# Key turns and key products stay in the stage that forms the systems; values, queries and scores move under the small blocks' transfers

## The chip, the core and the metric

The kernel runs on one core of a Trainium2 chip. A time is the device time of one execution in microseconds; three executions of the kernel before took 2998.97, 3002.99 and 3005.89 us, median 3002.99. Five engines work side by side, each in the order of its own list of instructions: TensorE (PE in the rows; its weight loads are PEld), VectorE (DVE), ScalarE (ACT), GpSimd (POOL) and SyncE (SP), which issues most of the DMA transfers. They wait for one another on semaphores. An instruction that waits holds back everything behind it on its engine.

## The reference, cut to what matters

A first block (a gated delta rule and a pooling mixer on 512 tokens and 256 context tokens, width 1024) and two transformer layers behind it. The change lies in the delta rule, which runs over 8 heads of 128 channels, forward and backward:

```python
hn = _rms_norm(h, gain) * (1 + scale) + shift
proj = jnp.einsum('bld,dp->blp', hn, w_in)
qkv = jax.nn.silu(_short_conv(qkv, conv_w))       # five taps
q, k = _l2_norm(q), _l2_norm(k)
...
# _gated_delta_rule, in chunks of tokens
decay = jnp.exp(jnp.where(incl, g[..., :, None] - g[..., None, :], -jnp.inf))
a_mat = jnp.where(strict, jnp.einsum('bhncd,bhnsd->bhncs', kb, k) * decay, 0.0)
sol = lax.linalg.triangular_solve(eye + a_mat, rhs, left_side=True, lower=True,
                                  unit_diagonal=True)
qk = jnp.einsum('bhncd,bhnsd->bhncs', q, k) * decay
...
def step(state, inp):
    v_new = u_i - jnp.einsum('bhcd,bhdv->bhcv', w_i, state)
    o_i = (jnp.einsum('bhcd,bhdv->bhcv', q_i, state)
           + jnp.einsum('bhcs,bhsv->bhcv', qk_i, v_new))
    state = state * jnp.exp(gl_i)[..., None, None] + jnp.einsum('bhcd,bhcv->bhdv', k_i, v_new)
```

## The kernel before, in words

The heads go in four groups of two (`GROUPS`), and each group has six tiles of 128 tokens (`TILES`): four of the sequence, two of the context. Channels lie on the partitions, so keys, values and queries have to be turned, tile by tile, before tokens lie there. All large products are made of three matmuls on split numbers (L149 to L151: high by high, high by low, low by high); the weights come in slabs by DMA, ScalarE rounds a slab (`split_hi`, L137) and VectorE makes the rest (`split_lo`, L142).

A group G runs through these stages.

1. *Systems.* For each tile TensorE sums the rows of the decay (L1589, L1591 in `rows`), turns keys and, in the first four tiles, queries into bank 3 and values into bank 7 (`turn_heads`, L1573 and L1578), multiplies keys by keys and by queries into bank 5 or 6 (`products`, L1601), and runs one part of a projection. ScalarE makes the exponentials (`decays`, L861), squares and copies of the turned keys, and the copy of the values (`squares`, L847 to L852). VectorE sums the squares (`norms`), multiplies scores (`scores`, kept as `qkd`) and systems (`system`, L1194, kept as `bt`).
2. *Small blocks.* SyncE sends the diagonal blocks of the systems to memory (L636) and back in another shape (L641); VectorE inverts them there in 15 rounds of four operations (`invert`, L1234 and L1240); SyncE sends the inverses out (L648) and in (L653). Meanwhile TensorE runs the rest of `fill`, the projections of group G+1 (part by part, `take(fill, 99)`), then `busy`, sixteen matmuls of no result (L1416), and then `turn_inverse` (L1616) waits for the blocks.
3. *Sweep.* 18 steps (`STEPS_LEVEL`) of turn, product (L1654) and correction make the whole inverse out of the blocks. From step 13 on TensorE takes one part of `later`, the projections of group G+2, after each step. `conv_ops` on VectorE (L1152) and `act_head`/`act_center` on ScalarE (L768 to L791) make the short convolution of group G+1 between these steps.
4. *Scan.* Six steps over the tiles, the first within the sweep: `against` and `answer` multiply the state, VectorE makes the residual (L1284) and the new state (L1295), TensorE `renew`, `grow` (L1679, L1688) and `inner` (the scores by the new values, L1719), with parts of `later` between them. At the end TensorE waits for the outputs (`oa_ready`, `ot_ready`) and goes to the next group.

The order is written out by hand. Semaphores hold the dependences: `vs_ready` counts the values that ScalarE has copied out of bank 7, and the next tile's value turn waits for it; `bt_ready` counts the systems; `qkd_ready` the scores, which are first read in `inner`; `bounce` counts the transfers of the blocks, and `dve_step` VectorE's own steps. In the stage of the small blocks ScalarE runs `act_raw`, `act_head`, `act_center` for group G+1 (L137, L768 to L791; in the last group a gate, `act_gate`, stands there), then the root of the key norms (L877, behind a table load) and the clearing of banks 5 and 6 (L880), which hold the key products till then.

GpSimd multiplies the values and the keys for the scan (L1835 to L1840), once the group's values are there.

Of the kernel before, what the change touches and what calls it, by code (L numbers as in the profile page):

```python
# [9 lines left out]
F32 = mybir.dt.float32  # L10
# [36 lines left out]
EPS = 1e-6  # L47
# [107 lines left out]
def make_layer_memory(nc, K, at):  # L155

    def put(name, shape, dtype=F32, where=None):
# [4 lines left out]
        if where is None:  # L162
# [112 lines left out]
HALF_SEMS = {"sum_made": ("tk_ready", 24), "sumh_ready": ("tv_ready", 24), "suml_ready": ("hsq_ready", 24), "plain_ready": ("hss_ready", 24),  # L275
             "diff_made": ("arg_ready", 24), "diffh_ready": ("dec_ready", 24), "diff_ready": ("kk_ready", 24),
# [125 lines left out]
NORM_STEPS = 2 * TILES + 1  # L402
# [52 lines left out]
def make_first_memory(nc, K, at):  # L455
# [64 lines left out]
    at += 2048  # L520

# [18 lines left out]
    K.junk = put("square_junk", [128, 4, 128])  # L540
    at += 2048
# [69 lines left out]
def delta_block(K):  # L611
# [224 lines left out]
    def act_group(act, G):  # L836
# [4 lines left out]
        def squares(t):  # L841
            n = TILES * G + t
            w = 4 if t < 4 else 2
            act.wait_ge(S.tk_ready, n + 1)
            if n > 0:
                act.wait_ge(S.hss_ready, n)
            nc.scalar.activation(K.junk[:, 0:w, :], pb[3][:, 0:128 * w].rearrange("p (c v) -> p c v", v=128), ACT.Square)\  # L847
                .then_inc(S.hsq_ready, 1)
            nc.scalar.activation(K.ks[:, t, 0:2, :], pb[3][:, 0:256].rearrange("p (c v) -> p c v", v=128), ACT.Copy)\
                .then_inc(S.kt_ready, 1)  # L850
            act.wait_ge(S.tv_ready, n + 1)
            nc.scalar.activation(K.vs[:, t, :, :], pb[7][:, 0:256].rearrange("p (j v) -> p j v", v=128), ACT.Copy)\  # L852
                .then_inc(S.vs_ready, 1)

        def decays(t):
            n = TILES * G + t
            act.wait_ge(S.arg_ready, n + 1)
            act.wait_ge(S.bt_ready, n - 1 + CREDIT)
            for c in range(4):
                at = 8 * (c // 2) + 2 * G + c % 2  # L860
                last = nc.scalar.activation(K.decs[t % 2][:, c, :], pb[4][:, 128 * c:128 * c + 128], ACT.Exp,  # L861
                                            bias=K.ncum[:, t, at:at + 1])
            last.then_inc(S.dec_ready, 1)
# [72 lines left out]
        for i in range(STEPS_LEVEL):  # L936
# [7 lines left out]
            if more and i in (0, 12, 16):  # L944
                act_head(act, G + 1, {0: 1, 12: 2, 16: 3}[i])
            if more and i in (1, 13, 17):
                act_center(act, G + 1, {1: 3, 13: 4, 17: 5}[i])
        for n, (f, b, x) in enumerate(scan_steps()):
# [4 lines left out]
            if x is not None:  # L953
                state_out(x, (f, b))
            if more and n == 3:
# [207 lines left out]
    def dve_group(dve, G):  # L1163
# [5 lines left out]
        def norms(t):  # L1169
            n = TILES * G + t  # L1170
            w = 4 if t < 4 else 2
            dve.wait_ge(S.hsq_ready, n + 1)
            nc.vector.tensor_reduce(K.ssq[:, t, 0:w], K.junk[:, 0:w, :], AX.X, ALU.add).then_inc(S.hss_ready, 1)
            dve.wait_ge(S.hss_ready, n + 1)
            step.link(nc.vector.tensor_scalar(K.ssq[:, t, 0:w], K.ssq[:, t, 0:w], EPS, None, ALU.add))
            step.link(nc.vector.reciprocal(K.n2[:, t, :], K.ssq[:, t, 0:2]))

        def scores(t):
            n = TILES * G + t
            dve.wait_ge(S.dec_ready, n + 1)  # L1180
            dve.wait_ge(S.kk_ready, n + 1)
            for j in range(2):
                ins = nc.vector.scalar_tensor_tensor(out=quad(K.qkd[:, t, :, :])[:, :, j, :], in0=quad(K.decs[t % 2][:, :, :])[:, :, j, :],
                                                     scalar=K.n2[:, t, j:j + 1],
                                                     in1=wide(pb[5 + t % 2][:, 256 + 128 * j:384 + 128 * j], 1, 2),
# [3 lines left out]
        def system(t):  # L1189
            n = TILES * G + t  # L1190
            dve.wait_ge(S.dec_ready, n + 1)
            dve.wait_ge(S.kk_ready, n + 1)
            for j in range(2):
                ins = nc.vector.scalar_tensor_tensor(out=quad(K.bt[t][:, :, :])[:, :, j, :], in0=quad(K.decs[t % 2][:, :, :])[:, :, j, :],  # L1194
# [6 lines left out]
        for t in range(TILES):  # L1201
            norms(t)
            if t < 4:
                scores(t)
# [4 lines left out]
                                wide(K.n2[:, :, :], 2, 2), ALU.mult).then_inc(S.tail_ready, 1)  # L1209
        step.link(nc.vector.tensor_scalar(K.fq[:, 2 * G:2 * G + 2, :].rearrange("p j t -> p t j"), K.ssq[:, 0:4, 2:4], 128 * EPS, None,  # L1210
                                          ALU.mult))
        if more:
            take(conv, 4)
# [42 lines left out]
        for i in range(STEPS_LEVEL):  # L1256
# [13 lines left out]
            take(conv, 1)  # L1270
# [42 lines left out]
        for n, (f, b, x) in enumerate(scan_steps()):  # L1313
# [8 lines left out]
            if n == 4 and more:  # L1322
# [229 lines left out]
    def pe_group(pe, G, fills):  # L1552
        s, v = DN_SLAB + 6 * (G + 1), DN_EVIC + 6 * (G + 1)
        fill, later = fills[G], islice(fills[G + 1], 14 if G + 1 < GROUPS else 16)
# [10 lines left out]
        def turn_heads(t):  # L1565

            n = TILES * G + t
            lo = 128 * t
            if t > 0:
                pe.wait_ge(S.kt_ready, n)  # L1570
            for c in range(4 if t < 4 else 2):
                src = keys(G, c) if c < 2 else queries(G, c - 2)
                last = nc.tensor.transpose(pb[3][:, 128 * c:128 * c + 128], src[:, lo:lo + 128], K.ident[:, :])  # L1573
            last.then_inc(S.tk_ready, 1)
            if t > 0:
# [1727 lines left out]
```

## Time and profile before

| | |
|---|---|
| median of three executions | 3002.99 us |
| the profiled execution | 3003.65 us |
| its span, first to last instruction | 3001.3 us |
| granted TensorE clock, mean | 0.989 |
| TensorE busy | 2901.6 us, 97% of the span |
| VectorE, ScalarE, GpSimd busy | 71%, 46%, 15% |

The share of an engine is an average over all stages. TensorE's is so high that the span is read from its side: what it runs, and where it stands idle. A granted clock of 1.00 is the upper of TensorE's two levels (2.4 GHz), 0.50 the lower (1.2 GHz). The other engines are read only where TensorE waits for them. The four groups' system stages begin at 121.98, 240.02, 356.62 and 475.49 us of the span; the two layers that the change does not touch begin after the first block.

### The profile page before, as it was taken

What the parts mean: (1) busy time and instruction counts of PE and PEld (TensorE: products, weight loads), DVE (VectorE), ACT (ScalarE), POOL (GpSimd) and SP (SyncE); (2) the same over time, 40 slices, a digit from 0 to 9 for tenths busy, and PEclk for the clock granted to TensorE, in tenths of its full rate; (3) what the DMA queues carried; (4) which work ended last, traced back from release to release, by engine and by line L of the source; (5) the groups of instructions that cost most, each with busy time, mean ns of one, the idle gap of its engine ahead of it and who ended that gap; (6) DMA issues with size and microseconds to landing.
All of it is one profiled execution on the core that took longest, in us unless ns stands there. A gap on an engine that the chain in (4) does not pass through costs nothing.

```text
span 3001.3 us, 50795 instructions
## 1 busy us (share of the span) xinstructions
PE 2901.6 (97%) x18548; PEld 2497.8 (83%) x18548; DVE 2128.3 (71%) x3193; ACT 1394.4 (46%) x2305; POOL 455.7 (15%) x356
## 2 busy tenths in 40 slices
PE   7999999889999999999999999999999999999998
PEld 3888888777799988777799988799888777899886
DVE  5677676455699745987799745899547886899545
ACT  3645555454366522334456522566323334566322
POOL 0113112184600010000300012100110000200012
PEclk9999999999999999999999999999999999999998
DMA  6212022123222322232323323233223222323322
GB/s 258 64 42 63 24 55 61 34 84 116 98 98 98 105 96 81 93 96 77 99 98 106 107 97 109 72 105 111 88 88 97 94 78 85 105 98 112 106 95 73
DMA packets 97244, 275.09 MB, mean 92 GB/s; under 512 B 35712, under 2 KB 36864, under 8 KB 95760
## 3 DMA queue, kind: packets, MB, share of 16 engines
q1 hardware_dynamic: 94016, 267.89, 27.3%
q10 hardware_dynamic: 2768, 4.25, 0.5%
q8 instruction: 92, 1.51, 0.2%
q0 software_dynamic: 320, 1.05, 0.1%
q14 instruction: 48, 0.39, 0.0%
HBM read 267.88 MB, written 5.28 MB: 91 GB/s over the span
## 4 chain that ended last, share of the span: by engine, by line
PE 84%; DVE 6%; ACT 3%; issue 2%; DMA 0%; ACTq 0%; DVEq 0%; POOL 0%; SPq 0%; POOLq 0%
PE bank L149 16%; PE bank L151 16%; PE bank L150 16%; PE bank L2053 8%; PE bank L2054 8%; PE bank L2055 8%; PE bank L1616 1%; DVE weights_lo L142 1%; ACT weights_hi L137 1%; PE bank L1679 1%; PE bank L1630 1%; PE bank L2544 1%; PE bank L2565 1%; PE bank L2555 1%; DVE short_conv L1152 1%
## 5 line engine op out<-in xcount | busy, mean ns | idle before, releaser
L142 DVE TENSOR_TENSOR weights_lo<-weights_raw,weights_hi 128x1024 fp32r<-128x1024 f32 (+2 forms) x258 | 396.9, 1538 | 326.5 <-ACT weights_hi L137 323.2
L137 ACT ACTIVATE weights_hi<-weights_raw 128x1024 fp32r<-128x1024 f32 (+2 forms) x250 | 285.3, 1141 | 432.1 <-PE bank L151 425.1
L149 PE MATMUL bank<-x_hi,weights_hi 128*128 128x512 f32 x832 | 336.8, 405 | 4.7 <-DVE x_lo L1943 3.0
L151 PE MATMUL bank<-x_hi,weights_lo 128*128 128x512 f32 x832 | 326.4, 392 | 0.0
L150 PE MATMUL bank<-x_lo,weights_hi 128*128 128x512 f32 x832 | 325.3, 391 | 0.0
L2053 PE MATMUL bank<-sum_hi,block_hi 128*128 128x256 f32 x960 | 270.9, 282 | 4.6 <-ACT bank L2205 3.7
L150 PE MATMUL bank<-hidden_lo,weights_hi 128*128 128x512 f32 x704 | 273.9, 389 | 0.0
L149 PE MATMUL bank<-hidden_hi,weights_hi 128*128 128x512 f32 x704 | 273.9, 389 | 0.0
L151 PE MATMUL bank<-hidden_hi,weights_lo 128*128 128x512 f32 x704 | 273.9, 389 | 0.0
L2054 PE MATMUL bank<-sum_lo,block_hi 128*128 128x256 f32 x960 | 270.5, 282 | 0.0
L2055 PE MATMUL bank<-sum_hi,block_lo 128*128 128x256 f32 x960 | 269.2, 280 | 0.0
L149 PE MATMUL bank<-normed_hi,weights_hi 128*128 128x512 f32 (+1 forms) x512 | 196.2, 383 | 10.6 <-ACT grid L1004 7.0
L2053 PE MATMUL bank<-x_hi,block_hi 128*128 128x256 f32 x640 | 181.9, 284 | 13.7 <-DVE block_lo L2357 7.7
L149 PEld LDWEIGHTS bank<-x_hi,weights_hi 128*128 128x128 f32 x832 | 157.2, 189 | 39.3 <-issue 4.9
L150 PE MATMUL bank<-normed_lo,weights_hi 128*128 128x512 f32 (+1 forms) x512 | 188.1, 367 | 0.0
L151 PE MATMUL bank<-normed_hi,weights_lo 128*128 128x512 f32 (+1 forms) x512 | 188.0, 367 | 0.0
L2053 PEld LDWEIGHTS bank<-sum_hi,block_hi 128*128 128x128 f32 x960 | 181.3, 189 | 5.8 <-ACT bank L2205 4.4
L151 PEld LDWEIGHTS bank<-x_hi,weights_lo 128*128 128x128 f32 x832 | 156.8, 188 | 34.2
L150 PEld LDWEIGHTS bank<-x_lo,weights_hi 128*128 128x128 f32 x832 | 157.2, 189 | 31.1 <-issue 1.7
L2055 PEld LDWEIGHTS bank<-sum_hi,block_lo 128*128 128x128 f32 x960 | 181.5, 189 | 0.0
L2054 PEld LDWEIGHTS bank<-sum_lo,block_hi 128*128 128x128 f32 x960 | 181.2, 189 | 0.0
L2055 PE MATMUL bank<-x_hi,block_lo 128*128 128x256 f32 x640 | 180.9, 283 | 0.0
(436 smaller groups left out, 7323.8 us busy)
## 6 DMA issues: line engine op xcount, KB each, us to landing
raw_pair<-w_ff1in SPq DMA_DIRECT2D x42, 1024.0 KB, 4.9
raw_pair<-w_ff2in SPq DMA_DIRECT2D x42, 1024.0 KB, 4.9
weights_raw<-w_mix SPq DMA_DIRECT2D x72, 512.0 KB, 3.5
weights_raw<-w_ff1out SPq DMA_DIRECT2D x32, 704.0 KB, 4.1
weights_raw<-w_ff2out SPq DMA_DIRECT2D x32, 704.0 KB, 4.1
weights_raw<-w_tail SPq DMA_DIRECT2D x42, 512.0 KB, 3.6
mod_weights<-w_mod SPq DMA_DIRECT2D x6, 2048.0 KB, 16.7
weights_raw<-w_dn SPq DMA_DIRECT2D x24, 512.0 KB, 3.7
```

The lines of the kernel that those rows point to most:

```text
L137: nc.scalar.activation(K.wh[:, slot, 0:cols], K.raw[:, slot, 0:cols], ACT.Copy).then_inc(S.wh_ready, 1)
L142: nc.vector.tensor_tensor(K.wl[:, slot, 0:cols], K.raw[:, slot, 0:cols], K.wh[:, slot, 0:cols].bitcast(F32), ALU.subtract).then_inc(S.raw_ ...
L149: nc.tensor.matmul(out, K.wh[:, slot, a:b], xh, start=start, stop=False)
L150: nc.tensor.matmul(out, K.wh[:, slot, a:b], xl, start=False, stop=False)
L151: return nc.tensor.matmul(out, K.wl[:, slot, a:b], xh, start=False, stop=stop)
L1152: ins = nc.vector.scalar_tensor_tensor(out=acc[:, base + lo:base + hi], in0=K.hv[i][:, base + lo + k - 2:base + hi + k - 2], scalar=K.wk[: ...
L1616: last = nc.tensor.transpose(pb[turn_bank(i)][:, 128 * q:128 * q + 128], K.e[:, q, t, :], K.ident[:, :])
L1630: last = nc.tensor.matmul(pb[3 + i % 2][own, 64 * q:64 * q + 64], K.bl[t][own, q, :] if i < STEPS_FIRST else K.bt[t][own, q, own], K.dd[ow ...
L1679: last = nc.tensor.matmul(pb[scan_bank(n, d)][:, part(j)], K.e[:, c, t, :], K.rr[:, c, :] if n else K.vs[:, t, j, :], start=True, stop=True)
L2053: nc.tensor.matmul(out, hi[:, a], x[0][:, k, :], start=start and k == 0, stop=False, skip_group_check=True)
L2054: nc.tensor.matmul(out, hi[:, a], x[1][:, k, :], start=False, stop=False, skip_group_check=True)
L2055: last = nc.tensor.matmul(out, lo[:, a], x[0][:, k, :], start=False, stop=(k == 3), skip_group_check=True)
```

## The change

The stage of the systems keeps the row sums, the key turns (`turn_keys`) and the products of keys by keys. The turns of the values, the turns of the queries (now into bank 7 beside the values) and the products of keys by queries (now into banks 3 and 4) come after the sixth tile, each tile followed by one part of a projection. Therefore:

- ScalarE copies values and squares queries (`values`) after its first steps for group G+1, and not tile by tile.
- VectorE sums the squared queries between convolution steps, and multiplies the scores after the inversion. The decays of the four sequence tiles stay in `qkd` until then.
- TensorE waits for the last value copy before the sixteen filler matmuls and for the scores before it turns the inverse.
- The waits for the outputs at a group's end move into the next group, before the first key product and before the first value turn.
- In the first two groups 20 parts of later projections are kept for the sweep and the scan, not 14 (in the third 16, before 14; in the last 16 as before); the sweep takes them from step 12 on, the scan at other places. Convolution steps on VectorE and ScalarE move within the sweep and the scan, on VectorE ahead of the new state.

```diff
@@ act_group
+        def values(t):
+            n = TILES * G + t
             act.wait_ge(S.tv_ready, n + 1)
+            if t < 4:
+                if t > 1:
+                    act.wait_ge(S.dve_step, (NORM_STEPS + SMALL_STEPS) * G + 2 * TILES + t - 1)
+                nc.scalar.activation(K.qsq[:, t % 2, :, :], pb[7][:, 256:512].rearrange("p (j v) -> p j v", v=128), ACT.Square)\
+                    .then_inc(S.hsq_ready, 1)
             nc.scalar.activation(K.vs[:, t, :, :], pb[7][:, 0:256].rearrange("p (j v) -> p j v", v=128), ACT.Copy)\
                 .then_inc(S.vs_ready, 1)
...
             act_center(act, G + 1, 1)
         else:
             act_gate(act, 1)
+        act.wait_ge(S.bt_ready, TILES * G + TILES + CREDIT)
+        for t in range(TILES):
+            values(t)
         act.wait_ge(S.dve_step, (NORM_STEPS + SMALL_STEPS) * G + 2 * TILES)
         nc.scalar.activation(K.knorm[:, :, :], K.ssq[:, :, 0:2], ACT.Sqrt).then_inc(S.knorm_ready, 1)
-        act.wait_ge(S.bt_ready, TILES * G + TILES + CREDIT)
@@ dve_group
         for t in range(TILES):
             norms(t)
-            if t < 4:
-                scores(t)
             system(t)
...
+        for t in range(4):
+            take(conv, 1)
+            query_sums(t)
...
-        if more:
-            take(conv, 4)
         split_lo(dve, s + 2, 0, 1024)
...
-            take(conv, 8)
         else:
             split_lo(dve, s + 5, 1, 1024)
+        dve.wait_ge(S.kk_ready, (TILES + 1) * (G + 1))
+        for t in range(4):
+            scores(t)
+        take(conv, 2)
...
-            take(conv, 1)
+            take(conv, 1 if i < STEPS_INNER else 2)
...
             if n < 5:
+                take(conv, 3 if n < 3 else 2)
                 new_state(n, (f, b))
-                take(conv, 3 if n < 3 else 2)
@@ pe_group
-        fill, later = fills[G], islice(fills[G + 1], 14 if G + 1 < GROUPS else 16)
+        fill, later = fills[G], islice(fills[G + 1], 20 if G + 2 < GROUPS else 16)
...
         for t in range(TILES):
             rows(t)
-            turn_heads(t)
+            turn_keys(t)
+            if t == 0 and G > 0:
+                pe.wait_ge(S.oa_ready, 4 * G)
             products(t)
             take(fill, 2 if G == 0 and t < 2 else 1)
+        if G > 0:
+            pe.wait_ge(S.ot_ready, 8 * G)
+        for t in range(TILES):
+            turn_rest(t)
+            take(fill, 1)
+            if t == 2:
+                pe.wait_ge(S.kt_ready, TILES * (G + 1))
+                pe.wait_ge(S.dec_ready, TILES * (G + 1))
+            if t > 1:
+                query_products(t - 2)
         take(fill, 99)
+        pe.wait_ge(S.vs_ready, TILES * (G + 1))
         busy(pe, pb[turn_bank(0)], 8)
+        pe.wait_ge(S.qkd_ready, 4 * (G + 1))
         for i in range(3):
             turn_inverse(i)
...
-            if i > STEPS_INNER:
+            if i >= STEPS_INNER:
                 take(later, 1)
```

The order of TensorE's list in the second group, from the row sums of its sixth tile on; `head_v` holds the values, `keys_queries` keys and queries, the three rows L149 to L151 are one part of a projection. Before:

```order
L1589 MATMUL bank<-sum_rows_141,row_pairs 128x128 [waits dec_ready]
L1589 MATMUL bank<-sum_rows_141,row_pairs 128x128 x3
L1591 MATMUL bank<-not_included,identity_r 128x512
L1573 MATMUL bank<-identity,keys_queries_175 128x128 [waits kt_ready]
L1573 MATMUL bank<-identity,keys_queries_175 128x128
L1578 MATMUL bank<-identity,head_v 128x128 [waits vs_ready]
L1578 MATMUL bank<-identity,head_v 128x128
L1601 MATMUL bank<-keys_queries_175 128x128 [waits bt_ready]
L1601 MATMUL bank<-keys_queries_175 128x128
L149 MATMUL bank<-normed_hi,weights_hi 128x256
```

From here on the projections ran without other work in between. After the change the list goes on, behind the key products of the same tile, with:

```order
L1630 MATMUL bank<-keys_queries_175 128x128
L149 MATMUL bank<-normed_hi,weights_hi 128x512
L150 MATMUL bank<-normed_lo,weights_hi 128x512
L151 MATMUL bank<-normed_hi,weights_lo 128x512
L1594 MATMUL bank<-identity,head_v 128x128 [waits ot_ready]
L1594 MATMUL bank<-identity,head_v 128x128
L1598 MATMUL bank<-identity,keys_queries_175 128x128 x2
L149 MATMUL bank<-normed_hi,weights_hi 128x512
L150 MATMUL bank<-normed_lo,weights_hi 128x512
L151 MATMUL bank<-normed_hi,weights_lo 128x512
L1594 MATMUL bank<-identity,head_v 128x128 [waits vs_ready]
L1594 MATMUL bank<-identity,head_v 128x128
```

The value turns left the tile and stand behind the projection part, four transposes at a time for values and queries, with the wait on the copied values at the second of them.

ScalarE's list in the same group, from the squared keys of the sixth tile on; `head_k`, `head_q` and `short_conv` belong to the convolution of the next group. Before:

```order
L847 ACTIVATE square_junk<-bank 128x256 [waits hss_ready,tk_ready]
L849 ACTIVATE decayed_keys<-bank 128x256
L852 ACTIVATE values<-bank 128x256 [waits tv_ready]
L137 ACTIVATE weights_hi<-weights_raw 128x1024 [waits slab_done,raw_full1]
L768 ACTIVATE head_k<-bank 128x512 [waits slab_done]
L770 ACTIVATE head_k<-bank 128x256
L791 ACTIVATE short_conv_206<-head_q,short_taps 128x512 [waits evac,head_ready]
L791 ACTIVATE short_conv_207<-head_k,short_taps 128x768 [waits evac,head_ready]
L877 ACT_TABLE_LOAD
L877 ACTIVATE key_norm<-head_squares 128x12 [waits dve_step]
```

Every tile's values were copied right behind its keys. Now, from the same place:

```order
L849 ACTIVATE decayed_keys<-bank 128x256
L137 ACTIVATE weights_hi<-weights_raw 128x1024 [waits slab_done,raw_full1]
L769 ACTIVATE head_k<-bank 128x512 [waits slab_done]
L771 ACTIVATE head_k<-bank 128x256
L792 ACTIVATE short_conv_207<-head_q,short_taps 128x512 [waits evac,head_ready]
L792 ACTIVATE short_conv_208<-head_k,short_taps 128x768 [waits evac,head_ready]
L857 ACTIVATE query_squares<-bank 128x256 [waits tv_ready,bt_ready]
L859 ACTIVATE values<-bank 128x256
L857 ACTIVATE query_squares<-bank 128x256 [waits tv_ready]
L859 ACTIVATE values<-bank 128x256
```

All six value copies stand behind the five steps for the next group and ahead of the table load and the key norms.

## Rows read from the trace of the kernel before

**Rows 1.** Page, busy time, share of the span and instructions of each engine.

```profile
PE 2901.6 (97%) x18548; PEld 2497.8 (83%) x18548; DVE 2128.3 (71%) x3193; ACT 1394.4 (46%) x2305; POOL 455.7 (15%) x356
```

**Rows 2.** Timeline, TensorE: start us, us, line, out<-in, count [idle before <-releaser].

```profile
255.68 0.66 PE L1589 MATMUL bank<-sum_rows,row_pairs 32*128 32x128 f32 x4
...
256.82 0.38 PE L1578 MATMUL bank<-identity,head_v 128*128 128x128 f32 x2
257.04 0.61 PE L1601 MATMUL bank<-keys_queries 128*128 128x128 f32 x4
257.40 0.36 PE L149 MATMUL bank<-normed_hi,weights_hi 128*128 128x256 f32 x1
```

**Rows 3.** Timeline, TensorE, end of the projections.

```profile
288.69 1.95 PE L1416 MATMUL bank<-ones 128*128 128x128 f32 x16
290.47 1.47 PE L1616 MATMUL bank<-identity,inverse 128*128 128x128 f32 x12
```

**Rows 4.** Timeline, SyncE's DMA queue, 262 to 290: time of issuing.

```profile
279.56 0.30 SPq L648 DMA_DIRECT2D inverse_blocks<-small_inverse  x1
283.38 2.60 SPq L653 DMA_DIRECT2D inverse<-inverse_blocks  x4
286.03 1.44 SPq L625 DMA_DIRECT2D weights_raw<-w_dn  x2
```

**Rows 5.** Waits, TensorE, 290.4 to 356.7: us in total, times, longest.

```profile
PE bank L1679 <- DVE residual L1284: 2.3, 3, 1.2
PE bank L1589 <- issue: 0.9, 1, 0.9
PE bank L1719 <- ACT new_values L922: 0.6, 1, 0.6
```

**Rows 6.** Windows: length, each engine's busy us (instructions), granted clock, DMA share, GB/s.

```profile
240.00:243.40 3.40, 3.38 (x23) 2.85 (x24) 0.63 (x1) 2.36 (x8) 3.14 (x3) 1.00 0.27 70
...
357.20:360.60 3.40, 3.40 (x16) 3.22 (x16) 0.90 (x2) 2.17 (x7) 2.50 (x3) 0.50 0.27 82
360.60:364.00 3.40, 3.40 (x25) 2.86 (x25) 2.89 (x6) 1.41 (x5) 1.34 (x2) 1.00 0.23 36
473.20:480.00 6.80, 5.91 (x28) 5.34 (x26) 1.73 (x4) 4.03 (x11) 3.66 (x4) 0.50 0.14 35
```

**Rows 7.** Timeline, TensorE, one projection part in the sweep.

```profile
322.90 0.48 PE L149 MATMUL bank<-normed_hi,weights_hi 128*128 128x512 f32 x1
323.22 0.39 PE L150 MATMUL bank<-normed_lo,weights_hi 128*128 128x512 f32 x1
323.45 0.40 PE L151 MATMUL bank<-normed_hi,weights_lo 128*128 128x512 f32 x1
323.77 0.45 PE L1654 MATMUL bank<-inverse,product 64*64 64x64 f32 x8
```

**Rows 8.** Timeline, ScalarE, from the sixth tile's exponentials on.

```profile
256.80 1.14 ACT L861 ACTIVATE decay_odd<-bank,log_beta_less_sum 128x128 f32<-128x128 f32 x4 [0.65 <-PE bank L1591]
...
258.34 0.42 ACT L852 ACTIVATE values<-bank 128x256 f32<-128x256 f32 x1
258.61 1.10 ACT L137 ACTIVATE weights_hi<-weights_raw 128x1024 fp32r<-128x1024 f32 x1
...
260.91 1.00 ACT L791 ACTIVATE short_conv<-head_k,short_taps 128x768 f32<-128x768 f32 x1
261.92 1.28 ACT L877 ACT_TABLE_LOAD   x1
...
263.34 1.10 ACT L880 ACTIVATE bank<-identity 128x512 f32<-128x512 f32 x2
```

**Rows 9.** Timeline, VectorE: last system, inversion, a split, convolution steps.

```profile
259.41 0.87 DVE L1194 SCALAR_TENSOR_TENSOR system<-decay_odd,key_square_inverse,bank 128x256 f32<-128x256 f32 x2
...
269.53 0.32 DVE L1234 TENSOR_TENSOR small_product<-small_system,small_inverse 48x30 f32<-48x30 f32 x2 [0.41 <-DMA small_system<-system_blocks]
...
284.58 2.51 DVE L142 TENSOR_TENSOR weights_lo<-weights_raw,weights_hi 128x1024 fp32r<-128x1024 f32 x1 [3.92 <-ACT weights_hi L137]
...
330.56 1.80 DVE L1152 SCALAR_TENSOR_TENSOR short_conv<-head_v,short_taps,short_conv 128x511 f32<-128x511 f32 x3
```

**Rows 10.** Timeline, GpSimd, its last multiplication of the group.

```profile
286.08 3.63 POOL L1840 TENSOR_TENSOR decayed_keys<-decayed_keys,tail_by_square 128x1536 f32<-128x1536 f32 x1
```

More of the change, by code:

```diff
@@ L539, in make_first_memory @@
     K.decs = [K.dec, put("decay_odd", [128, 4, 128])]
-    K.junk = put("square_junk", [128, 4, 128])
-    at += 2048
+    K.junk = put("square_junk", [128, 2, 128])
+    at += 3072
     end = at
@@ L954, in act_group @@
                 state_out(x, (f, b))
+            if more and n == 1:
+                act_center(act, G + 1, 5)
             if more and n == 3:
@@ L1319, in dve_group @@
             if n < 5:
+                take(conv, 3 if n < 3 else 2)
                 new_state(n, (f, b))
-                take(conv, 3 if n < 3 else 2)
-            if n == 4 and more:
+            elif more:
                 split_lo(dve, s + 6, 0, 1024)
@@ L1577, in turn_heads, with query_products @@
             for j in range(2):
-                last = nc.tensor.transpose(pb[7][:, 128 * j:128 * j + 128], K.hv[HEAD_SLABS.index((2, j))][:, lo:lo + 128], K.ident[:, :])
-            last.then_inc(S.tv_ready, 1)
+                last = nc.tensor.transpose(pb[7][:, 128 * j:128 * j + 128], K.hv[HEAD_SLABS.index((2, j))][:, 128 * t:128 * t + 128],
+                                           K.ident[:, :])
+            if t < 4:
+                for j in range(2):
+                    last = nc.tensor.transpose(pb[7][:, 256 + 128 * j:384 + 128 * j], queries(G, j)[:, 128 * t:128 * t + 128],
+                                               K.ident[:, :])
+            last.then_inc(S.tv_ready, 1)
+        def query_products(t):
+            for j in range(2):
+                a = 256 * (t % 2) + 128 * j
+                last = nc.tensor.matmul(pb[3 + t // 2][:, a:a + 128], keys(G, j)[:, 128 * t:128 * t + 128],
+                                        queries(G, j)[:, 128 * t:128 * t + 128], start=True, stop=True)
+            if t == 3:
+                last.then_inc(S.kk_ready, 1)
         def rows(t):
@@ L1597, in products @@
                 pe.wait_ge(S.bt_ready, n - 1 + CREDIT)
-            lo = 128 * t
             for j in range(2):
-                key = keys(G, j)[:, lo:lo + 128]
+                key = keys(G, j)[:, 128 * t:128 * t + 128]
                 last = nc.tensor.matmul(pb[5 + t % 2][:, 128 * j:128 * j + 128], key, key, start=True, stop=True)
-                if t < 4:
-                    last = nc.tensor.matmul(pb[5 + t % 2][:, 256 + 128 * j:384 + 128 * j], key, queries(G, j)[:, lo:lo + 128],
-                                            start=True, stop=True)
             last.then_inc(S.kk_ready, 1)
@@ L1741, in pe_group @@
                 against(n, d, t)
-            if x is None:
-                take(later, 1)
-            else:
+            if x is not None:
                 answer(n, x, tiles)
+            take(later, 1)
             if n == 1:
@@ L1749, in pe_group @@
                 renew(n, d, t)
-            take(later, 2)
+            take(later, 2 if n in (2, 3, 4) else 1)
             if n < 5:
@@ L1753, in pe_group @@
                     grow(n, d, t)
-            if x is not None:
-                if x == 0:
-                    pe.wait_ge(S.qkd_ready, 4 * G + 4)
+            if x is None:
+                take(later, 1)
+            else:
                 inner(n, x, tiles)
-        pe.wait_ge(S.oa_ready, 4 * G + 4)
-        pe.wait_ge(S.ot_ready, 8 * G + 8)
     def pe_tail(pe):
+        pe.wait_ge(S.oa_ready, 4 * GROUPS)
+        pe.wait_ge(S.ot_ready, 8 * GROUPS)
         for i, (kind, m) in LATE:
```

63 lines of the change are left out of this document (31 added, 32 removed).

## The prediction

> **What bounds the kernel.** I read the page's engine shares first. TensorE is busy in 97% of the span [rows 1], so the time is its instructions plus the holes between them; another engine counts only where it makes a hole or a slower clock. I then read one of the four head groups, the second, in order of time; the others have the same pattern. All offsets below count from 255.68, where TensorE begins the row sums of that group's sixth and last tile [rows 2].
>
> After that tile TensorE runs projection products of the next group without a hole until 288.69, sixteen filler products until 290.47, and then turns the inverse [rows 3]. No idle time stands before 290.47, so the small blocks were back by then: VectorE's inversion ended at 279.56, the block loads were issued by 285.98 [rows 4]. The transfers are hidden today. The reader should look for holes elsewhere, and the view of waits has them: in the group's sweep TensorE stands idle 2.3 us for residuals, 0.6 for new values and 0.9 at the border to the next group [rows 5]. After two of the borders the granted clock is at 0.50, the lower of the two levels, once for 3.4 us and once for 6.8; in such a stretch 16 matmuls ran where the next 3.4 us held 25 [rows 6].
>
> **The change part by part.** TensorE's matmuls are the same in number and shape; only their order changes. So I add up holes, breaks and clock.
>
> *The shorter stage.* Two value turns, two query turns and two query products leave each of the first four tiles, two value turns each of the last two. That is no gain: TensorE still has to run them before it turns the inverse, and it was TensorE, not the transfers, that arrived there last.
>
> *The new wait.* Values share one bank, so the second tile's value turn waits until ScalarE has copied the first. In the last tile TensorE reaches the projection part at +1.72; less 0.22 for the value turns that left [rows 2] it is +1.50. One part of a projection takes 0.87 (322.90 to 323.77) [rows 7], the first turn of values and queries (four transposes, twice 0.22) 0.44, a second part 0.87: TensorE wants the second turn at +3.68. ScalarE has its exponentials at +1.12, then two copies, then a weight split, the copy of the next group's key projection and two centre steps, and ends these at 261.92, which is +6.24; without the value copy that stood among them (0.27, 258.34 to 258.61) it is +5.97 [rows 8]. Only then come the first query squares (0.26, like the copy) and the first values (0.42): +6.65. The hole is 6.65 - 3.68 = 3.0 us. Queued behind the waiting turn are all later turns, the query products and 37 parts of projections. Later tiles alternate without a hole worth counting: TensorE's 1.31 to 1.75 us a tile cover ScalarE's 0.7. In the last group a gate with a table load stands in place of the copies and centres; I take 3.0 there too. Four groups: 12.0 us. The bounds are 2.2 (ScalarE one step earlier) and 3.9 each.
>
> *Breaks in the projections.* Three products at the drain's pitch take 0.69 (323.22 to 323.45 is 0.23), a part by itself takes 0.87 [rows 7], so a part set between other work costs up to 0.18 that it does not cost in a row. The change breaks out six more parts a group under the transfers and in the sweeps 7, 7, 4 and 3: 45 places. At 0 to 0.18 each that is 0 to 8.1; what follows them is of other kinds than in the row, so I take 0.15: 6.8 us.
>
> *The transfers' and the scores' chains, at nothing.* TensorE leaves the value stage at 6.65 + 1.31 + 2 x 1.75 + 2 x 1.53 = +14.5, runs 32 parts of 0.69 (+36.6) and the filler of 1.78 (+38.4). The inversion today starts on its data at 269.53, +13.85 [rows 9]; now it stands on VectorE behind a weight split whose first half ScalarE makes only after the last values (+13.8), the table load, norms and bank clearing (2.52, 261.92 to 264.44) and 1.10 for itself [rows 8]: +17.4, with VectorE's half +18.6. Its 10.0 us and about 9.0 for the blocks' way out and in (between 6.4 and 10.9 by rows 3 and 4) give +37.6. So the head start of the shorter stage is lost on that wait, and the blocks arrive 0.8 before TensorE. The scores now stand after the inversion and after a split that needs the fifth projection, done 5.5 before the drain ends (+31.1): ScalarE 1.1, VectorE 1.2 to 2.5, eight score operations at 0.43 (the systems' two took 0.87 [rows 9]) end at +36.9 to +38.2. TensorE's new wait on them costs nothing while it arrives at +38.4, and whatever exceeds this if it comes sooner.
>
> VectorE's split took 2.51 us at 284.58 [rows 9], and GpSimd's last multiplication began at 286.08 and ended at 289.71 [rows 10]: the two disturb each other, and the scores now fall in just that time. The Trainium skill (SBUF — State Buffer, section "SBUF: two separate sides") says that GpSimd and VectorE hold one port pair by turns, for a whole instruction, and that of VectorE's instructions those in a two-port mode or with two SBUF inputs need it. A score has one input from PSUM, so by that rule it is not held, and the sum stays; without the rule the second rival below would be as likely as not.
>
> *The sweep.* Of the 3.8 us of holes named above, each understated by the 0.16 by which a matmul's recorded end overlaps the next start (256.82 + 0.38 against 257.04 [rows 2]), five times: 4.6 us. The convolution steps on VectorE now run before the new state instead of between it and the next residual (three of them took 1.80 [rows 9]), the fifth step gets two parts, and the waits at the border go. Left over: about 1.6 at the first scan step, where two convolutions instead of one precede each residual (0.6 more, twice over), and 0.5 for a copy and a centre on ScalarE that move into its busiest steps (0 to 1.8; a centre is 1.00 [rows 8]). Net -2.5 in groups one and two; in the third the parts run out before the fifth step, -1.5; in the last, which has 16 parts as before but none in the fifth step, +0.6 by the same count. Together -5.9 us, bounds -11 and +1.
>
> *The clock.* The three low stretches at the borders lost 9 of 25 matmuls in 3.4 us, 1.2 each: -3.7 if the holes before them go. But a 3.0 us hole is longer than any single hole at those borders (1.2 the longest [rows 5]), so I expect one low stretch in each group after it: 4 x 1.2 = +4.8.
>
> Sum: 12.0 + 6.8 - 5.9 - 3.7 + 4.8 = +14.0 us. The profiled execution took 3003.65, 0.66 above the median of 3002.99 and inside the runs' 2998.97 to 3005.89; so 3017.0 on the median's scale.
>
> **Rivals.**
> 1. *Not slower: the wait at the second value turn does not arise,* since ScalarE has room to spare (46% busy). Then 12.0 and its 4.8 of clock go: 14.0 - 16.8 = -2.8, 3000.2. It decides where ScalarE's first value copy ends before +3.7. Against it: ScalarE works in order and its row from 258.61 to 261.92 has no idle time. Chance 0.13, a part of it below 2997.
> 2. *The scores come last.* If GpSimd holds them, they start when its multiplications end, 10.1 us after the inversion (289.71 against 279.56 [rows 4, 10]): +38.7, done at +42.2, 3.8 later than TensorE: 4 x 3.8 = +15 more, 3032. Chance 0.07.
> 3. *The hole leaves the clock alone.* For it: the border between the first two groups has the same waits and no low stretch after it [rows 6]. 14.0 - 4.8 = +9.2, 3012.2. Chance 0.20.
> 4. *The earlier blocks let TensorE turn sooner,* as the change's words suggest. TensorE would have to do without work it still has; I give it 0.05 with what I have not seen, some of it faster.
>
> **How the numbers follow.** The forecast has 0.55 and its own range of 3010 to 3024 (breaks and sweep at their ends). The range for 8 in 10 runs from 3000, which cuts rival 1 in the middle, to 3028, which leaves out rival 2. About 6 us, 0.2%, is what a measurement here can tell from no change: faster takes half of rival 1 and some of 4, 0.10; same takes the other half, the low ends of rival 3 and of the forecast, 0.18; slower the rest, 0.72.
>
> **What would show it.** Right: in each group an idle stretch of TensorE of about 3 us before a turn of values, released by ScalarE's value copy, a low clock after it; the inversion starting on a weight split instead of its data; TensorE turning the inverse about 38 us after the last tile's row sums began, where it was 34.8; no idle time at the borders. Wrong: no such stretch; or a hole before the inverse's first turn, released by scores or blocks, which would make a chain, not TensorE, the bound there.

## The result, and the profile after

The changed kernel takes 3012.59 us (median of six, 3011.41 to 3016.20), the kernel before beside it 3001.16: ratio 1.0039, interval 1.0027 to 1.0051. It is slower by 11.4 us; 14.0 were forecast. The profiled execution has a span of 3010.6 at a mean clock of 0.990. TensorE is as busy as before, and no other engine's busy time moved by more than 6 us [rows 1]:

```profile
PE 2901.5 (96%) x18548; PEld 2492.3 (83%) x18548; DVE 2128.7 (71%) x3213; ACT 1397.6 (46%) x2321; POOL 459.1 (15%) x356
```

From the first row sums of the first group to TensorE's last product of the fourth it was 468.07 us and is 478.21. So 10.1 us lie there; the two profiled executions differ by 9.3 over their whole spans, the medians by 11.4. What TensorE waits for in the second group (245.3 to 364.3; total, times, longest) answers to [rows 5]:

```profile
PE bank L1594 <- ACT values L859: 3.0, 1, 3.0
PE bank L1719 <- DVE residual L1298: 1.6, 1, 1.6
PE bank L1642 <- DVE decayed_scores L1195: 0.8, 1, 0.8
PE bank L1656 <- issue: 0.3, 1, 0.3
```

The waits at the border and for the later residuals are gone; the wait at the value turn has come, and so has one for the scores. TensorE in that place (the sixth tile's row sums begin at 257.73), against [rows 2]:

```profile
260.02 0.38 PE L1594 MATMUL bank<-identity,head_v 128*128 128x128 f32 x2
260.24 0.38 PE L1598 MATMUL bank<-identity,keys_queries 128*128 128x128 f32 x2
260.37 0.48 PE L149 MATMUL bank<-normed_hi,weights_hi 128*128 128x512 f32 x1
...
260.92 0.40 PE L151 MATMUL bank<-normed_hi,weights_lo 128*128 128x512 f32 x1
264.27 0.44 PE L1594 MATMUL bank<-identity,head_v 128*128 128x128 f32 x2 [2.96 <-ACT values L859]
```

and ScalarE, against [rows 8]:

```profile
260.39 1.09 ACT L137 ACTIVATE weights_hi<-weights_raw 128x1024 fp32r<-128x1024 f32 x1
261.34 0.63 ACT L769 ACTIVATE head_k<-bank 128x512 f32<-128x512 f32 x1
261.81 0.43 ACT L771 ACTIVATE head_k<-bank 128x256 f32<-128x256 f32 x1
262.08 0.77 ACT L792 ACTIVATE short_conv<-head_q,short_taps 128x512 f32<-128x512 f32 x1
262.69 0.98 ACT L792 ACTIVATE short_conv<-head_k,short_taps 128x768 f32<-128x768 f32 x1
263.51 0.43 ACT L857 ACTIVATE query_squares<-bank 128x256 f32<-128x256 f32 x1
263.78 0.44 ACT L859 ACTIVATE values<-bank 128x256 f32<-128x256 f32 x1
```

ScalarE works without a gap, and the values stand last. The hole is 2.96 us in three groups and 2.68 in the last. The clock behind it, in windows as in [rows 6] (the first is of group one, 384 and 500 of groups three and four, 514 behind a second hole of group four):

```profile
143.60:147.00 3.40, 3.35 (x23) 2.74 (x24) 3.20 (x7) 1.32 (x4) 0.99 (x1) 1.00 0.65 211
...
264.80:268.20 3.40, 3.40 (x17) 2.98 (x16) 2.69 (x5) 1.32 (x4) 0.23 (x1) 0.53 0.99 247
268.40:271.80 3.40, 3.40 (x32) 3.40 (x31) 0.90 (x4) 1.05 (x3) 0.00 (x0) 1.00 0.15 23
384.40:387.80 3.40, 3.34 (x16) 3.14 (x16) 2.50 (x5) 0.86 (x3) 0.00 (x0) 0.51 0.86 246
500.40:503.80 3.40, 3.40 (x13) 2.87 (x14) 0.51 (x2) 1.06 (x4) 0.51 (x1) 0.52 0.70 196
514.00:517.40 3.40, 3.40 (x9) 2.62 (x10) 2.58 (x12) 1.28 (x2) 0.00 (x0) 0.53 0.61 175
```

At the end of the stage, VectorE, against [rows 9]:

```profile
276.02 1.23 DVE L142 TENSOR_TENSOR weights_lo<-weights_raw,weights_hi 128x1024 fp32r<-128x1024 f32 x1 [5.50 <-ACT weights_hi L137]
277.17 0.32 DVE L1245 TENSOR_TENSOR small_product<-small_system,small_inverse 48x30 f32<-48x30 f32 x2
...
291.04 3.69 DVE L142 TENSOR_TENSOR weights_lo<-weights_raw,weights_hi 128x1024 fp32r<-128x1024 f32 x1 [2.74 <-ACT weights_hi L137]
294.65 3.21 DVE L1195 SCALAR_TENSOR_TENSOR decayed_scores<-decayed_scores,key_square_inverse,bank 128x256 f32<-128x256 f32 x8
```

GpSimd's last two multiplications, against [rows 10], and TensorE's turn of the inverse, against [rows 3]:

```profile
290.88 2.76 POOL L1877 TENSOR_TENSOR decayed_keys<-decayed_keys,tail_by_square 128x1536 f32<-128x1536 f32 x1
293.72 3.62 POOL L1879 TENSOR_TENSOR decayed_keys<-decayed_keys,tail_by_square 128x1536 f32<-128x1536 f32 x1
```

```profile
295.15 1.95 PE L1430 MATMUL bank<-ones 128*128 128x128 f32 x16
297.92 1.31 PE L1642 MATMUL bank<-identity,inverse 128*128 128x128 f32 x10 [0.82 <-DVE decayed_scores L1195]
```

The inversion starts at +19.4, right behind a split that ScalarE released late; TensorE turns the inverse at +40.2 (before: +34.8), held by the scores for the last 0.8.

### The profile page after: what moved, and what is told of

Same layout as the page of the kernel before. It is cut to its first block, busy times and chain, and to the rows that moved or that the text cites. A ratio compares the mean times of both kernels' runs of the same rounds, so it can differ in the third digit from the quotient of the medians.

```text
span 3010.6 us, 50813 instructions
## 1 busy us (share of the span) xinstructions
PE 2901.5 (96%) x18548; PEld 2492.3 (83%) x18548; DVE 2128.7 (71%) x3213; ACT 1397.6 (46%) x2321; POOL 459.1 (15%) x356
## 4 chain that ended last, share of the span: by engine, by line
PE 85%; DVE 6%; ACT 5%; issue 2%; SPq 1%; DMA 1%; ACTq 0%; DVEq 0%; POOL 0%; POOLq 0%
PE bank L149 16%; PE bank L151 16%; PE bank L150 16%; PE bank L2092 8%; PE bank L2093 8%; PE bank L2094 8%; PE bank L1642 1%; ACT weights_hi L137 1%; DVE weights_lo L142 1%; SPq L671 1%; PE bank L2583 1%; PE bank L1719 1%; PE bank L1656 1%; PE bank L1728 1%; PE bank L2604 1%
## 5 line engine op out<-in xcount | busy, mean ns | idle before, releaser
L149 PE MATMUL bank<-x_hi,weights_hi 128*128 128x512 f32 x832 | 337.0, 405 | 4.4 <-DVE x_lo L1982 2.7
L151 PE MATMUL bank<-x_hi,weights_lo 128*128 128x512 f32 x832 | 326.4, 392 | 0.0
L149 PE MATMUL bank<-hidden_hi,weights_hi 128*128 128x512 f32 x704 | 273.9, 389 | 0.0
L151 PE MATMUL bank<-hidden_hi,weights_lo 128*128 128x512 f32 x704 | 273.9, 389 | 0.0
L149 PE MATMUL bank<-normed_hi,weights_hi 128*128 128x512 f32 (+1 forms) x512 | 202.1, 395 | 11.5 <-ACT grid L1014 7.0
L149 PEld LDWEIGHTS bank<-x_hi,weights_hi 128*128 128x128 f32 x832 | 157.3, 189 | 39.4 <-issue 4.8
L151 PE MATMUL bank<-normed_hi,weights_lo 128*128 128x512 f32 (+1 forms) x512 | 189.8, 371 | 0.0
L151 PEld LDWEIGHTS bank<-x_hi,weights_lo 128*128 128x128 f32 x832 | 156.7, 188 | 34.1
L2092 PE MATMUL bank<-x_hi,plain_block_hi 128*128 128x256 f32 x640 | 179.8, 281 | 0.8 <-DVE plain_block_lo L2401 0.8
```

What stands on the lines that cost most here:

```text
L149: nc.tensor.matmul(out, K.wh[:, slot, a:b], xh, start=start, stop=False)
L151: return nc.tensor.matmul(out, K.wl[:, slot, a:b], xh, start=False, stop=stop)
L2092: nc.tensor.matmul(out, hi[:, a], x[0][:, k, :], start=start and k == 0, stop=False, skip_group_check=True)
```

## The experiments

All times are medians of 5 to 12 executions, with the 95% interval of the ratio to the kernel before, which ran beside them (its medians there: 3002.4 to 3003.6, single executions 2997 to 3010). A difference between two of these kernels is therefore sure to a few us only; where the traces give it too, both are named.

**The hole taken out.**

```diff
+        values(0)
         if more:
-            act_raw(act, G + 1, 1)
+            values(1)
+            split_hi(act, DN_SLAB + 6 * G + 9, 1, 1024)
+            values(2)
+            act_raw(act, G + 1, 1, True)
+            values(3)
             act_center(act, G + 1, 0)
+            values(4)
             act_center(act, G + 1, 1)
+            values(5)
...
-        for t in range(TILES):
-            values(t)
```

(`act_raw` with True is its copies alone, without the split. The cut parts give the query squares another buffer, let VectorE sum two of them earlier, and set the last group's values between its split and its gate.)

> The changed kernel, with ScalarE's six value copies set between its steps for the next group and ahead of the key norms, and the query squares in a buffer that need not wait for the systems. My theory (the 3 us hole before the second value turn is ScalarE's order, nothing else): the hole of 2.7 to 3.0 us in each of the four groups goes, and with it the low clock stretch behind it in three of them; 3012.6 - 12.2 - 3.9 = 2996.5 (2993 to 3001). The scores' wait of 0.8 us stays in groups two and three, since TensorE and VectorE both come 3 us earlier. Rival (the hole is only the first of several limits: the next projection slab or the inversion is then late): holes of 2 us or more turn up elsewhere in the stage, 3006 to 3012.

Measured: 3002.33, ratio 0.9998 (0.9990 to 1.0007), 10.3 less than the changed kernel. The hole is gone and no low stretch stands behind its place, but a shorter wait took over behind the third value turn (TensorE, second group; 1.6 in the third too, and 1.35 for a split in the last):

```profile
PE bank L149 <- ACT head_k L771: 1.6, 1, 1.6
PE bank L1730 <- DVE residual L1309: 1.6, 1, 1.6
PE bank L1653 <- DVE decayed_scores L1204: 0.8, 1, 0.8
```

The next slab's part for the context tiles needs the bank that ScalarE's copy of the key projection, now behind the values, sets free. So ScalarE's order is the cause, as the theory has it; that the hole would simply go was wrong by 6 us, and the rival of a next limit is right in kind, at less than its price.

**The hole alone, in the kernel before.**

```diff
             take(fill, 2 if G == 0 and t < 2 else 1)
+        if G + 1 < GROUPS:
+            pe.wait_ge(S.center_ready, 6 * G + 8)
+        else:
+            pe.wait_ge(S.evac, v + 2 + CREDIT)
         take(fill, 99)
```

> The kernel before, with one wait added: behind the sixth tile's projection part TensorE waits until ScalarE has ended its second centre step (in the last group its gate). Nothing else is moved. Theory (a hole there is paid in full, since no work of TensorE is waiting elsewhere, and its clock on top): 3 x 3.6 + 2.7 = 13.5 us of holes and about 4 us of low clock, 3018.5. Rival 1 (paid in full, but the clock costs nothing on the sum): 3014.7. Rival 2 (the hole is made good at the turn of the inverse, where the blocks set the time): 3001.

Measured: 3018.90, 1.0051 (1.0037 to 1.0066), 16.2 more than before. The holes are 3.59 three times and 3.32, and a low stretch of 3.4 to 6.8 us goes with each of the four (second group):

```profile
PE bank L149 <- ACT short_conv L791: 3.6, 1, 3.6
PE bank L1683 <- DVE residual L1284: 2.3, 3, 1.2
```

A hole there is paid in full, with its clock on top; the turn of the inverse gives nothing back. In the traces the four groups take 17.2 us more: 14.7 are the holes with an overlap of 0.16 each. The low stretches behind the borders of the kernel before, 4.3 us as shown below, are missing here, so that the clock of the four new ones comes to some 6.8. The sum came out as the theory had it partly by luck, since it had left the borders alone.

**The hole filled with work of no result.**

```diff
             turn_rest(t)
             take(fill, 1)
+            if t == 0:
+                pe.wait_ge(S.kt_ready, TILES * (G + 1))
+                busy(pe, pb[3], 25)
```

(in a second kernel 13).

> The changed kernel, with 25 filler matmuls (2.8 us at the upper clock level) on TensorE ahead of the second value turn of each group, where it stood idle for 2.96 us; every wait stays as long. Theory A (the low clock behind the hole comes from TensorE's idle time there): the low stretches at about 265, 384 and 500 go, the one behind the gate of the last group at 514 stays; 3 x 1.3 = 4 us less, 3008.5. Theory B (the idle time does not set the clock there): the low stretches stay where they are, 3012.6. In both the second value turn comes no earlier than now.

> The changed kernel with 13 filler matmuls ahead of the second value turn instead of 25: the 25 took 5.6 us in a hole of 2.96, so that they cost 2.6 us a group; 13 take 2.9. Theory (idle time there brings the low clock): no low stretch behind the value turns, the one behind the last group's gate gone as with 25; 3012.6 less 4 x 1.5 = 3006.6 (3005 to 3009). Rival (25 fillers kept the clock up only since they ran on past the hole): low stretches as in the changed kernel, 3012.6.

With 25: 3018.71 (1.0036 to 1.0067), a miss, since each filler stands in the trace as two matmuls of 0.11 us (50 in all), so that they took 5.6 us in a hole of 3.0. With 13: 3007.60 (1.0012 to 1.0032). In both no stretch of the four groups is low. The 13 fillers, the window behind them, and the one behind the second hole of the last group:

```profile
494.60:498.00 3.40, 3.40 (x32) 3.40 (x31) 3.00 (x6) 2.75 (x5) 2.92 (x3) 1.00 0.20 32
498.00:501.40 3.40, 3.36 (x22) 2.66 (x22) 0.84 (x2) 1.61 (x6) 0.04 (x1) 1.00 0.62 184
509.80:513.20 3.40, 3.40 (x15) 2.84 (x16) 2.59 (x12) 1.27 (x2) 0.00 (x0) 1.00 0.60 176
```

The second value turn comes as late as ever (+6.55, in the changed kernel +6.54), so 3012.59 - 3007.60 = 5.0 us is the clock's share of the change; by the two traces it is 5.7 over the four groups. That the stretch behind the gate goes too was not what theory A had said for 25.

**The sweep's part alone.**

```diff
             if n < 5:
+                take(conv, 3 if n < 3 else 2)
                 new_state(n, (f, b))
-                take(conv, 3 if n < 3 else 2)
...
-        fill, later = fills[G], islice(fills[G + 1], 14 if G + 1 < GROUPS else 16)
+        fill, later = fills[G], islice(fills[G + 1], 20 if G + 2 < GROUPS else 16)
...
-            if i > STEPS_INNER:
+            if i >= STEPS_INNER:
                 take(later, 1)
...
```

> The kernel before, with the change's sweep, scan and border only (convolution steps ahead of the new state, 20 later parts in the first two groups and 16 in the others at the changed places, the waits for outputs behind the next group's first row sums and key turns); the stage that forms the systems, the scores and the small blocks as before. By the terms of the prediction: -5.9 of holes, -3.7 of clock, +3 for breaks, 2994.5. By the trace of the changed kernel, in which the scans of the first three groups lost 5.0, 5.0 and 4.3 us beside their projection parts: about -14, 2987. Rival (the gain needs the moved stage): 3001.

Measured: 2989.88, 0.9959 (0.9945 to 0.9973), 12.8 less than before. So the change is two changes: a sweep that gains 13 us and a moved stage that costs 23 (22 by the traces). What moved with the stage is counted with it: the convolution steps that VectorE and ScalarE did under the transfers before stay there in this kernel.

**Which line of the sweep.**

```diff
             if n < 5:
+                take(conv, 3 if n < 3 else 2)
                 new_state(n, (f, b))
-                take(conv, 3 if n < 3 else 2)
```

> The kernel before with VectorE's list alone changed in the scan: the convolution steps ahead of the new state, not behind it. Theory A (the scan's gain is that a residual no longer stands behind convolution steps): most of the holes before residuals go, 1.19 in each of three groups; the hole before the first residual of the scan stays; the gain is 5 to 8 of the 13 us, 2995 to 2998. Theory B (the gain is the work that now stands between the scan's steps): nothing, or the new states come later and TensorE waits for them, 3001 to 3004.

Measured: 2988.21, 0.9963 (0.9950 to 0.9977): this line alone gives 14 us, more than either theory, and the rest of the sweep's part nothing that the times show. VectorE between the fifth and the sixth step of the second group's scan, before (the last residual stands behind two convolution steps and a split):

```profile
348.53 1.12 DVE L1295 SCALAR_TENSOR_TENSOR state<-state,chunk_decay,bank 128x128 f32<-128x128 f32 x4 [1.97 <-PE bank L1688]
349.57 1.53 DVE L1152 SCALAR_TENSOR_TENSOR short_conv<-head_q,short_taps,short_conv 128x511 f32<-128x511 f32 x2
351.01 1.22 DVE L142 TENSOR_TENSOR weights_lo<-weights_raw,weights_hi 128x1024 fp32r<-128x1024 f32 x1
352.15 1.12 DVE L1284 SCALAR_TENSOR_TENSOR residual<-bank,minus_exp_sum,values 128x128 f32<-128x128 f32 x4
```

With the line moved, the convolution steps are done while VectorE would wait for the new state's input, and the residual stands behind the split alone:

```profile
343.14 1.12 DVE L1295 SCALAR_TENSOR_TENSOR state<-state,chunk_decay,bank 128x128 f32<-128x128 f32 x4 [0.83 <-PE bank L1688]
344.19 1.23 DVE L142 TENSOR_TENSOR weights_lo<-weights_raw,weights_hi 128x1024 fp32r<-128x1024 f32 x1
345.33 1.12 DVE L1284 SCALAR_TENSOR_TENSOR residual<-bank,minus_exp_sum,values 128x128 f32<-128x128 f32 x4
```

TensorE's waits in the second group, against [rows 5]:

```profile
PE bank L1589 <- issue: 0.9, 1, 0.9
PE bank L1719 <- ACT new_values L922: 0.6, 1, 0.6
PE bank L1679 <- DVE residual L1284: 0.5, 1, 0.5
```

Beside its projection parts the scan of a group takes 22.4 us instead of 25.6, three times. TensorE's list is the same in both kernels, so the 3.2 us can be placed: it gains them behind four residuals, 1.0, 0.4, 0.4 and 1.4 us, where the trace of before shows idle times of 0.64, 0.06, 0.06 and 1.19. The other 4.3 us are the low clock in the two traces, which is gone although the border's hole of 0.9 stays; the median execution has a mean clock of 0.992 here, 0.989 before.

**The moved stage without its waits.** The first experiment, with the key copies ahead of the second value copy, the scores ahead of the inversion, the last group's second gate ahead of the key norms, and one convolution step fewer before the first residual.

```diff
+        dve.wait_ge(S.kk_ready, (TILES + 1) * (G + 1))
+        for t in range(4):
+            scores(t)
         split_lo(dve, s + 2, 0, 1024)
...
-        dve.wait_ge(S.kk_ready, (TILES + 1) * (G + 1))
-        for t in range(4):
-            scores(t)
...
```

> The changed kernel with the waits that its stage makes taken out: value copies between ScalarE's other steps, the copies of the next group's key projection ahead of the second of them, scores ahead of the inversion (where VectorE stood idle for 5.5 us), the last group's second gate ahead of the key norms, and one convolution step instead of two before the first residual of the scan. From the kernel with the value copies alone moved (3002.3): holes of 1.6 x 2, 0.83 x 2, 2.08 with its low clock of 1.5, and 1.05 x 3 go, 3002.3 - 11.6 = 2990.7. Theory (the transfers were hidden already, so a shorter stage has nothing to give): no faster than the kernel with the sweep's part alone, 2989.9, and about 1 to 3 us slower for its breaks in the projections: 2988 to 2994. Rival (rid of its waits, the shorter stage pays): below 2985.

Measured: 2993.36, 0.9974 (0.9965 to 0.9984). In the second group two waits above 0.2 us are left:

```profile
PE bank L1731 <- DVE residual L1310: 1.2, 1, 1.2
PE bank L1668 <- issue: 0.3, 1, 0.3
```

The last group still waits 1.3 and 1.8 us for splits. Even so the kernel does not beat the sweep's part alone: from the first group's row sums to the last product of the fourth its trace takes 459.3 us, that of the sweep's part 456.0. The same projection parts, each counted up to the next start and without idle time, take 196.8 and 193.5 us in the two; all the rest, idle time included, takes 261.8 and 261.9. So the moved stage, rid of most of its waits, gives nothing and costs the breaks in its projections.

**Holes of the sweep's part closed.**

```diff
-            act_raw(act, G + 1, 1)
+            act_raw(act, G + 1, 1, True)
+            split_hi(act, DN_SLAB + 6 * G + 9, 1, 1024)
...
             act_gate(act, 1)
+            act_gate(act, 2)
```

> The kernel before with the sweep's part of the change (2989.9), and with two of the holes that it has in the projections closed: the copies of the next group's key projection ahead of the weight split (0.79 us in groups two and three), the last group's second gate ahead of the key norms (2.03 us). Theory (each hole of TensorE counts in full): 2989.9 - 3.6 - the overlap of 0.16 each = 2986. Rival (the next split or evacuation is late in turn): 2989 to 2990.

Measured: 2989.81, 0.9965 (0.9953 to 0.9977): the rival. The gate's hole of 2.0 stays (it is the first gate that TensorE waits for there, not the second). In the second group the wait for the key copies is gone, but the next split comes 1.55 late where it came 0.62 late; in the third a split comes late, and then the blocks:

```profile
PE bank L149 <- DVE weights_lo L142: 0.9, 1, 0.9
PE bank L1621 <- DMA inverse<-inverse_blocks: 0.8, 1, 0.8
```

In the first two groups six parts were put off to the sweep, so the projections of the second and third are that much shorter. In the third group the transfers are then the last to arrive, here and, by 0.48 us, in the sweep's part alone.

**A version that beats both.** The line on VectorE, and the border's waits moved; then a fifteenth part.

```diff
+            elif G > 0:
+                pe.wait_ge(S.ot_ready, 8 * G)
+                pe.wait_ge(S.oa_ready, 4 * G)
...
-        pe.wait_ge(S.oa_ready, 4 * G + 4)
-        pe.wait_ge(S.ot_ready, 8 * G + 8)
```

> The kernel before with the convolution steps ahead of the new state (2988.2), and the waits for the outputs at a group's end moved behind the next group's first row sums and key turns. Theory (each hole of TensorE counts in full): the hole of 0.89 at three borders goes, with the overlap of 0.16 each, 2985.0. Rival (the wait only moves to the first value turn): 2988.

> The same with a fifteenth part of later projections in the first three groups, which stands between the last renewal and the last scores' product of the scan, where TensorE waits 0.56 us for the new values. Theory: the three holes go, 3 x (0.56 + 0.16) less 3 x 0.1 for the break, 2983. Rival (what the part hides there it costs at the next group's turn of the inverse, where the drain is one part shorter): 2985, or more.

Measured: 2986.52 and 2985.81, both 0.9944 (0.9929 to 0.9959): some 17 us faster than before. The first lies between theory and rival, the second at its rival's time, and the times do not tell the two apart. In their traces the second and third groups take 112.48 and 111.81 us each from border to border, where the line alone takes 113.41: the holes do go. The last group of the second kernel waits 1.35 for its gate instead of 0.67, which takes a part of it back.

## Why the prediction was right, step by step

**The new wait: right.** 12.0 were forecast (3.0 a group); measured 11.56, and 0.16 more for each by the overlap, 12.2. The rival that it does not arise fell. So did the fourth: TensorE turns the inverse later, not sooner.

**The clock: right in sum.** +4.8 forecast for four stretches behind the hole, 5.0 by the filler. That the count is four is luck: one of them stands behind a second hole of the last group, which the prediction did not have, and group one has none, as the third rival said for all. The border's stretches gave back 4.3 (3.7 forecast): without projection parts the tiles of groups three and four took 1.6 and 2.1 us more than those of group two before, and the scan of group three 0.6.

**Breaks: a little less.** In the kernel with 13 fillers, whose groups run at the upper level, projection parts take about 5.5 us more than in the kernel before: 0.12 for each of 45 places, where I took 0.15.

**The sweep: mis-sized, the one large error.** Net -5.9 was forecast. Without projection parts and clock the scans gave 5.0, 5.0, 3.7 and -0.3 us, 13.4 in all. The 1.6 left over at the first scan step is there (1.55). What failed is the count of what goes: I took 4.6 a group, the idle time that the view of waits shows and 0.16 for five of them. Waits shorter than the overlap show no idle time and were left out: without its projection parts and the border's clock a scan of before took 25.64 us (4.15 of them idle), 6.6 more than the 19.08 that the same instructions take in the changed kernel beside their one idle time of 1.55.

**What was missing.** The scores, whose cost was put at nothing: I gave them +36.9 to +38.2 and they ended at +40.1. The split before them began at +33.3, 1.1 later than in the working, and took 3.69 us beside GpSimd, not 1.2 to 2.5; TensorE waited 0.8 for the scores in two groups. The last group's projections wait 2.08 for its second gate, which ScalarE reaches only behind the values, where they waited 0.67 for a split before. The first group's tiles wait 0.7 for exponentials, and the sweeps take 0.6 more. With these the terms add to 12.2 + 5.5 - 13.4 - 4.3 + 5.0 + 1.9 + 1.4 + 0.7 + 0.6 = 9.6 (10.3 with the 5.7 of the traces for the clock), and 10.1 were measured over the four groups.

So the forecast held by mechanism where it had one, and in size partly because a gain taken too small stood against costs left out. The second rival's wait (scores last) exists, but at a tenth of its price, 1.6 us instead of 15: the scores took 0.40 us each beside GpSimd's multiplication (294.65 and 293.72), so they are not held by it. The split, which has two inputs in SBUF, is: it began at 291.04 and ended 1.09 us behind GpSimd's multiplication of 290.88 to 293.64, and alone it takes 1.23 (276.02). The Trainium skill (SBUF — State Buffer, section "SBUF: two separate sides") states that a VectorE instruction with two SBUF inputs and a GpSimd instruction that reads SBUF share a lock, held for a whole instruction, so that the later one waits for the other's end. The trace agrees, and that of before does too: there the split of 284.58 ended at 287.09, 1.08 us behind the multiplication ahead of the one that the prediction names:

```profile
283.25 2.76 POOL L1838 TENSOR_TENSOR decayed_keys<-decayed_keys,tail_by_square 128x1536 f32<-128x1536 f32 x1
```

GpSimd's multiplications fall on this split because they start behind the inversion (287.25), not as soon as the values are there.

## What to carry to other kernels

Where one engine is busy 97% of the time, read its list for places where it waits, and split a change by such places: this one hid a line worth 14 us behind a move that costs 23. Moving work under a transfer gains nothing while the bound engine still arrives later than the transfer, and whatever is moved behind another engine's steps becomes a wait for them. Size a gain by the time between two instructions of the bound engine, not by the idle time shown: short waits show none.

## What the runs showed of the hardware

The clock fell after some holes of TensorE and not after others of the same length: after 2.96 us in groups two and three and not in group one; with 3.59 in group one of the kernel with the hole alone; and after the last group's first gate's hole of 2.03 us in one kernel and not in another. The windows behind that last hole, in the sweep's part alone and with its holes closed:

```profile
486.60:490.00 3.40, 3.40 (x15) 2.83 (x16) 0.15 (x2) 3.37 (x6) 0.75 (x2) 1.00 0.72 205
```

```profile
487.60:491.00 3.40, 3.40 (x9) 2.65 (x8) 0.92 (x1) 2.58 (x5) 0.00 (x0) 0.51 0.93 252
```

The borders of the kernel with the hole alone have the same waits as those of the kernel before, and no low stretch. Filling the holes at the value turn with matmuls kept the clock at 1.00 in all four groups, even after the last group's second gate's hole of 2.08, which was left open. So TensorE's idle time there brings the clock down, but what else decides stays open.
